# Second attention: the forget gates enter the scores by DMA, GpSimd and VectorE's maximum pass, not by TensorE products

## The reference

```
log_f = log_sigmoid(h @ w_f + b_f)            # one value per token and head
c     = cumsum(log_f, axis=tokens)
s     = (q * 64**-0.5) @ k.T + c[query] - c[key]
s     = where(key <= query, s, -1e30)
o     = softmax(s) @ v
```

## Time and profile before

| | us |
|---|---|
| median of 3 runs | 2159.78 |
| lowest, highest | 2157.82, 2160.03 |
| the profiled execution, device time | 2159.29 |
| its span on the core | 2157.5 |
| PE busy | 2127.7 (99%) |
| DVE busy | 1006.3 (47%) |
| ACT busy | 879.4 (41%) |
| POOL busy | 936.5 (43%) |

### The profile page before, as it was taken

How to read it: one execution, slowest core, us unless ns; L and a number is a source line. 1 busy time by engine, 2 the same in 40 slices (tenths; PEclk the granted TensorE clock), 3 DMA queues, 4 the chain that set the end, 5 groups by cost and what they waited for, 6 DMA issues and landing times.

```text
span 2157.5 us, 25220 instructions
## 1 busy us (share of the span) xinstructions
PE 2127.7 (99%) x10070; PEld 1739.1 (81%) x10070; DVE 1006.3 (47%) x1790; ACT 879.4 (41%) x1365; POOL 936.5 (43%) x424
## 2 busy tenths in 40 slices
PE   9999999999999999999999999999999999999998
PEld 7877778888888887777778888888888888888886
DVE  5887865265525235666635322314633254223134
ACT  5444455344424254555434422324522244223234
POOL 5632124444444455222235444445544454444446
PEclk9999999999999999999999999999999999999999
DMA  4421113333333332211122333332223323333322
GB/s 161 147 87 41 49 50 98 94 102 98 98 98 98 97 109 79 69 51 57 50 88 79 97 98 98 98 97 87 90 92 96 96 79 98 97 98 98 98 86 80
DMA packets 53829, 193.26 MB, mean 90 GB/s; under 512 B 6096, under 2 KB 6224, under 8 KB 53712
## 3 DMA queue, kind: packets, MB, share of 16 engines
q1 hardware_dynamic: 52992, 189.81, 28.3%
q10 hardware_dynamic: 720, 1.84, 0.3%
HBM read 189.53 MB, written 2.10 MB: 89 GB/s over the span
## 4 chain that ended last, share of the span: by engine, by line
PE 90%; DVE 5%; ACT 4%; issue 1%; POOL 0%; DMA 0%; DVEq 0%; ACTq 0%; POOLq 0%
PE ps L518 28%; PE ps L520 27%; PE ps L519 27%; PE ps L730 1%; ACT w_hi L1862 1%; PE ps L983 1%; PE ps L1002 1%; PE ps L722 1%; PE ps L712 1%; PE ps L614 1%; PE ps L1009 1%; DVE xg_lo L1173 1%; PE ps L1011 0%; PE ps L1010 0%; ACT fprob L2001 0%
## 5 line engine op out<-in xcount | busy, mean ns | idle before, releaser
L471 POOL TENSOR_TENSOR w_lo<-w_raw,w_hi 128x1024 fp32r<-128x1024 f32 x352 | 854.2, 2428 | 1182.6 <-ACT w_hi L1862 1182.5
L518 PE MATMUL ps<-xg_hi,w_hi 128*128 128x512 f32 x1688 | 675.1, 400 | 4.9 <-POOL w_lo L485 2.6
L520 PE MATMUL ps<-xg_hi,w_lo 128*128 128x512 f32 x1688 | 659.4, 391 | 0.0
L519 PE MATMUL ps<-xg_lo,w_hi 128*128 128x512 f32 x1688 | 658.7, 390 | 0.0
L1862 ACT ACTIVATE w_hi<-w_raw 128x1024 fp32r<-128x1024 f32 x352 | 372.0, 1057 | 626.1 <-PE ps L520 623.0
L518 PEld LDWEIGHTS ps<-xg_hi,w_hi 128*128 128x128 f32 x1688 | 317.6, 188 | 79.6 <-issue 12.4
L520 PEld LDWEIGHTS ps<-xg_hi,w_lo 128*128 128x128 f32 x1688 | 317.4, 188 | 68.0
L519 PEld LDWEIGHTS ps<-xg_lo,w_hi 128*128 128x128 f32 x1688 | 318.0, 188 | 59.6
L518 PE MATMUL ps<-h_hi,w_hi 128*128 128x512 f32 x688 | 267.6, 389 | 0.0
L519 PE MATMUL ps<-h_lo,w_hi 128*128 128x512 f32 x688 | 267.6, 389 | 0.0
L520 PE MATMUL ps<-h_hi,w_lo 128*128 128x512 f32 x688 | 267.6, 389 | 0.0
(11 more groups left out here) (342 smaller groups left out, 2425.3 us busy)
## 6 DMA issues: line engine op xcount, KB each, us to landing
w_raw<-in_weights SPq DMA_DIRECT2D x352, 512.0 KB, 3.5
out_x<-mixed SPq DMA_DIRECT2D x8, 256.0 KB, 2.1
resid<-in_x SPq DMA_DIRECT2D x3, 512.0 KB, 7.9
p_raw<-in_p ACTq DMA_DIRECT2D x3, 512.0 KB, 3.5
resid<-in_x SPq DMA_DIRECT2D x2, 256.0 KB, 4.2
last_gain<-in_last_gain SPq DMA_DIRECT2D x1, 512.0 KB, 4.4
w_raw<-in_weights SPq DMA_DIRECT2D x1, 256.0 KB, 3.6
w_raw<-in_weights ACTq DMA_DIRECT2D x1, 256.0 KB, 3.8
```

Source lines behind the costliest of these rows:

```text
L471: pool.tensor_tensor(w_lo[:, slot, :], w_raw[:, u % RAW, :], w_hi[:, slot, :].bitcast(F32), ALU.subtract).then_inc(w_ready, 1)
L518: pe.matmul(o, w, x, start=start, stop=False)
L519: pe.matmul(o, w, xl, start=False, stop=False)
L520: return pe.matmul(o, wl, x, start=False, stop=stop)
```

## The change

`c_head`, `c_hi`, `ones_r` and `head_sel` go, and with them everything that makes them. After the running sum ACT stores the 16 rows of `c_rows` to a tensor in device memory. For each pair, ACT then issues four DMAs (`gates_to_rows`), one for each query block: block qi reads the first (qi + 1) * 128 gates of both heads of the pair and writes them to all 128 partitions of `gate_row[:, :, qi]`, so that they end at column 512. For pair 0 that is ahead of ACT's work on units 144 and later; for pair p + 1 it stands where line 2270 stood. POOL adds the causal triangle to the last 128 columns of the eight rows of a partition in one operation (`gate_rows`), after it has waited for all four DMAs. It does so behind `low` of fixed units: behind unit fox + 6 for pair 0, and behind fox + 10, 13, 15, 18, 20, 23 and 25 for pairs 1 to 7 (fox is unit 141). DVE's `mx` takes `gate_row` in place of `causal`. The wait for `crow` moves from TensorE, ahead of `scores(0)`, to DVE, ahead of `mx(0)`. `scores` stops after its three products.

```diff
-        ones_r = sb("ones_r", [P, P], F32R)
...
-        head_sel = sb("head_sel", [P, 8], whole_lines=False)
...
-            c_hi = sb("c_hi", [P, S], F32R, fx)
-            c_head = sb("c_head", [P, S], F32R, fx)
+            gate_row = sb("gate_row", [P, 2, QB, S], scope=fx)
...
+        c_dram = nc.dram_tensor("c_dram", (16, S), F32, kind="Internal").ap()
...
-            pool.memset(head_sel[:], 0.0).then_inc(c_pool, 1)
...
-            for n, (first, base) in enumerate(((0, 0), (32, 0), (64, -1), (96, -1))):
-                rows = head_sel[first:first + 32, :]
-                pool.wait_ge(c_pool, 10 + n)
-                pool.affine_select(out=rows, in_=rows, compare_op=ALU.not_equal, fill=1.0, base=base,
-                                   pattern=[[-2, 8]], channel_multiplier=1).then_inc(c_pool, 1)
...
+            def gate_rows(p):
+
+                own_block = gate_row[:, :, :, S - P:S].rearrange("p h q s -> p (h q) s")
+                pool.wait_ge(A2["clanded"], 64 * (p + 1))
+                pool.tensor_tensor(own_block, own_block, causal[:, S - P:S].unsqueeze(1).to_broadcast([P, 2 * QB, P]),
+                                   ALU.add).then_inc(A2["crow"], 1)
+
+            gates_after = {U["fox"] + 6: 0, **{U["fox"] + fox_made(p, 3) // DC + RING: p + 1 for p in range(7)}}
...
                     low(u)
+                    if u in gates_after:
+                        gate_rows(gates_after[u])
...
-                            pe.matmul(ps[:, 2 + hd, 0:n], a[rows, :], b[rows, 0:n], start=t == 0, stop=False)
-                    for hd in range(2):
-                        rows = slice(hd * HD, (hd + 1) * HD)
-                        pe.matmul(ps[:, 2 + hd, 0:n], ones_r[rows, :], c_head[rows, 0:n], start=False, stop=True).then_inc(A2["scores"], 1)
+                            mm = pe.matmul(ps[:, 2 + hd, 0:n], a[rows, :], b[rows, 0:n], start=t == 0, stop=t == 2)
+                            if t == 2:
+                                mm.then_inc(A2["scores"], 1)
...
                 pe.wait_ge(bank_free, u0 + 3 * p + 2)
-                pe.wait_ge(A2["crow"], p + 1)
...
-            dve.wait_ge(s_fg["act"], 4)
-            dve.wait_ge(s_fg["dve"], 4)
-            for first in (32, 96):
-                rows = slice(first, first + 32)
-                low(c_rows[rows, :], c_rows[rows, :], c_hi[rows, :], s_fg["dve"])
-            dve.wait_ge(s_fg["dve"], 6)
-
-            dve.tensor_scalar(c_head[:], c_rows[:], head_sel[:, 0:1], None, ALU.mult).then_inc(A2["crow"], 1)
...
-                        masked_peak(A2, fstat, fprob, qi, hd)
+                        masked_peak(A2, fstat, fprob, qi, hd, gate_row[:, hd, qi, :])
...
+                dve.wait_ge(A2["crow"], p + 1)
                 mx(0)
...
-            act.activation(ones_r[:], ones[:], ACT.Copy).then_inc(c_act, 1)
...
+            def gates_to_rows(p):
+
+                for qi in range(QB):
+                    n = (qi + 1) * P
+                    act.dma_start(gate_row[:, :, qi, S - n:S], c_dram[2 * p:2 * p + 2, 0:n].unsqueeze(0).to_broadcast([P, 2, n])).then_inc(
+                        A2["clanded"], 16)
+
             act.wait_ge(s_fg["dve"], 4)
-            act.activation(c_hi[:], c_rows[:], ACT.Copy).then_inc(s_fg["act"], 1)
+            act.dma_start(c_dram, c_rows[0:16, :]).then_inc(c_stored, 16)
+            highs(u0 + 7)
+            act.wait_ge(c_stored, 16)
+            gates_to_rows(0)
...
                 if p < 7:
-                    act.activation(c_head[:], c_rows[:], ACT.Copy, scale=head_sel[:, p + 1:p + 2]).then_inc(A2["crow"], 1)
+                    gates_to_rows(p + 1)
```

More of the change, by code:

```diff
@@ L252, in build @@
         token = sb("token", [P, 14], whole_lines=False)
-        head_sel = sb("head_sel", [P, 8], whole_lines=False)
-        sb("rest_of_line", [P, 8], whole_lines=False)
+        sb("rest_of_line", [P, 16], whole_lines=False)
         m1 = ExitStack()
@@ L373, in build @@
         s_cs = stage_sems("cmp_att", "scores", "sub", "exp", "stat", "probs")
-        A2 = stage_sems("fox", *att_names, "qk", "qkhi", "vturned", "vhi", "vlo", "crow")
+        A2 = stage_sems("fox", *att_names, "qk", "qkhi", "vturned", "vhi", "vlo", "crow", "clanded")
+        c_stored = sem("c_stored")
+        c_dram = nc.dram_tensor("c_dram", (16, S), F32, kind="Internal").ap()
         s_fg = stage_sems("forget", "dve", "act")
@@ L441, in _ @@
             pool.memset(valid[:], 1.0).then_inc(c_pool, 1)
-            pool.memset(head_sel[:], 0.0).then_inc(c_pool, 1)
             pool.memset(own[:], 1.0).then_inc(c_pool, 1)
-            pool.wait_ge(c_pool, 6)
+            pool.wait_ge(c_pool, 5)
             pool.affine_select(out=ident[:], in_=ident[:], compare_op=ALU.not_equal, fill=1.0, base=0,
@@ L465, in _ @@
                                    pattern=[[0, HD]], channel_multiplier=(-1, 1)[g]).then_inc(c_pool, 1)
-            pool.wait_ge(c_pool, 16)
+            pool.wait_ge(c_pool, 11)
             def low(u):
@@ L630, in _ @@
                 pe.matmul(ps[:, 0, 0:P], ones[:], ones[:], start=True, stop=True)
-            pe.wait_ge(c_pool, 16)
+            pe.wait_ge(c_pool, 11)
             u0 = U["cmp_in"]
@@ L791, in values @@
                 head_values(A1, event(b) + kb, kb, vv_hi[:, :, b % 2], vv_lo[:, :, b % 2], b % 2 == 0 and kb == 0, b % 2 == 1 and kb == QB - 1)
-            pe.wait_ge(c_act, 4)
+            pe.wait_ge(c_act, 3)
             pe.wait_ge(s_kv["lo"], 6)
@@ L1190, in _ @@
             dve.wait_ge(gain_loaded, 16)
-            dve.wait_ge(c_pool, 16)
+            dve.wait_ge(c_pool, 11)
             for m in range(DC):
@@ L1320, in _, with masked_peak @@
             scaled(U["gates"], T[:, 0:1, :])
-            def masked_peak(A, st, pr, qi, hd):
+            def masked_peak(A, st, pr, qi, hd, mask):
                 n = (qi + 1) * P
-                dve.tensor_tensor_reduce(pr[:, hd, P_OFF[qi]:P_OFF[qi] + n], ps[:, 2 + hd, 0:n], causal[:, QB * P - n:], -1.0, BIG,
+                dve.tensor_tensor_reduce(pr[:, hd, P_OFF[qi]:P_OFF[qi] + n], ps[:, 2 + hd, 0:n], mask[:, QB * P - n:], -1.0, BIG,
                                          ALU.add, ALU.min, st[:, 0, hd, qi:qi + 1]).then_inc(A["peak"], 1)
@@ L1345, in head_peaks @@
                 for hd in range(2):
-                    masked_peak(A, st, probs, qi, hd)
+                    masked_peak(A, st, probs, qi, hd, causal)
             def head_normalise(A, s, qi, st, probs, gate=None):
@@ L1915, in _ @@
             act.wait_ge(vec_loaded, 16)
-            act.wait_ge(c_pool, 16)
+            act.wait_ge(c_pool, 11)
             highs(4)
```

## The result

The changed kernel takes 2170.8 us (median of 4, 2169.99 to 2173.09), the kernel before beside it 2158.8: a ratio of 1.0058, 95% interval 1.0046 to 1.0070, 12 us slower. The forecast was 2169 in a range of 2160.5 to 2178.

The account below looks back on a forecast made before the run. TensorE, with 90% of the chain of waits, was taken as the bound. -4.0 (products) + 4.9 (pair 0) + 5.6 (ACT's issues) + 2.8 (pair 2) = +9.3 us, 2169 on the median, range 2160.5 to 2178.

Parts of the forecast that it names:

- the three losses: Pair 0's chain to the first maximum 4.9 us, ACT's four issues 5.6, POOL's late add in pair 2 2.8.
- The gate products: TensorE's stream: dropping them saves 0.62 us a pair, 5.0 for eight, of which 4.0 is kept.
- The start of the program: POOL's dropped memset and selections and DVE's dropped head work gain 0 us, 0.3 if misjudged.
- Pair 0: Store, gate DMAs and POOL's add make the first maximum 3.9 us late; one caught scaling adds 1.0; together 4.9.
- ACT's issues: Four issues per pair replace one copy, delaying w_hi by 1.0 us in pairs 0, 1, 2, 3, 5; sum 5.6.
- Pair 2: POOL's add behind fox + 13 comes late, the first maximum waits 3.6 us, TensorE loses 2.8.
- The other pairs' adds: POOL's adds from pair 3 on come ahead of need or within TensorE's slack: 0 us.
- The rival in which issues and gates hide: ACT issues cost 2.0 us, gates land at 882 (0.9), pair 2 stays (2.8): 2161.5; chance 0.17.
- The rival in which the products are all there is: TensorE's stream alone decides, new arrivals fit its slack, 5.0 us gained: 2154.8; chance 0.05.
- The slow one: Packet-bound gates landing at 891 or issues of twice the length: +15 or +21, 2175 to 2181 us; chance 0.16.
- A maximum pass slower for its other mask: DVE's maximum pass loses from reading another mask; same shapes in SBUF, so no chance of its own.

Follow-up runs that it names:

- e1: Kernel before with only the fourth (gate) product left out of the scores, c_head still made: 2156.6 us, ratio 0.9991.
- e2: Changed kernel with POOL's add for pair 2 one unit earlier, behind fox + 12 in place of fox + 13: 2166.3 us.
- e4: Changed kernel with POOL's add for pair 0 behind the low half of fox + 8 in place of fox + 6: 2168.9 us.
- e5: Changed kernel with pair 0's add in four parts, each waiting for its own DMA, each maximum only for its part: 2167.5 us.
- e3: Changed kernel with the 28 gate DMAs of pairs 1 to 7 issued from SyncE's queue in place of ACT's: 2166.1 us.
- e8: Changed kernel with 13 idle matmuls filling TensorE's wait ahead of the second scores of pair 0: 2169.6 us.
- e6: Changed kernel with the changes of e2, e3 and e5 together: 2158.9 us, ratio 1.0003 to the kernel before.
- e9: Changed kernel, but pair 0 keeps the fourth product; pairs 1 to 7's gate DMAs issued by SyncE, pair 2's add one unit earlier: 2156.7 us, ratio 0.9990.

## Why the prediction was right

The forecast was +9.3, the result +12.0, within the range and of the right sign. The sign was earned: each of the three losses that it named was found in its place. Set out as its terms, the distances give -1.8 for the products (e1), +6.7 in pair 0, +3.1 for all else that the change adds in pairs 1 to 6 (e2 against e1), and +3.9 for the late place in pair 2 with its clock (changed against e2), 11.9 of 12.0. By its own steps:

- **The gate products, 4.0 gained: mis-sized.** e1 gives 1.7. The groups do leave the stream at 0.11 to 0.23 us each, and TensorE is 0.66 ahead by the end of the scores. Its error lies in taking this saving for kept: I had struck only the places where TensorE already waited for a maximum, and not asked whether the probabilities and turned blocks behind the scores would come earlier too. In pair 1 they came 0.66 - 0.42 = 0.24 less early than the scores, for DVE's scaling ran into POOL's `low`. Pairs 1, 2, 4 and 5 were to give 0.62 each and gave 0.3, 0.7, 0.4 and 0.3; pair 2, with no collision and no wait, is the only one that kept all.
- **The start of the program, 0: right.** The first scores stood at 882.1 to 883.4 in all profiles, with and without the selections.
- **Pair 0, 4.9 by itself, 5.7 with its ACT share and kept saving: right in kind, 6.7 measured.** The first maximum came at 887.11, with the program 0.9 ahead of the kernel before, so 4.3 late where I said 3.9: the store landed after 1.6 and not 2.1, the gates 9.1 after the first issue and not 7.8, the add took 2.35 and not 2.7. Of scalings caught by a `low` I counted one, 1.0 us; two were caught, 1.0 and 1.7. e4 (0.29 each) and e5 (one caught) show that cause. Of the 6.7, 0.8 belong to the one profile; e2, e3 and e8 have 5.9, which is nearer to the 5.7.
- **ACT's issues, 5.6 (its parts add to 5.7): right in kind, too high.** `w_hi` comes 1.93 - 1.32 = 0.61 later than before, where I said 1.0, because the sequencer issues the first two ahead. Against no copy and no issue it is 1.23, and that is what e3 took back in pairs 3 and 5. The forecast was against the copy, and there the runs give about half: TensorE's waits for the low half of turned probabilities grow by 2.4 (3.7 to 6.1, where I said about 9), and of the 3.1 above about 2 are such waits, 0.6 each in pairs 2, 3 and 5. Pair 1, for which I had said 1.0, gives 0.1 to 0.2. That there is next to nothing in pair 4 came as said.
- **Pair 2, 2.8: right, but for the clock.** 3.0 by e3 against e6, for the reason given, and 0.9 more for the clock, which the prediction left out altogether. The text ahead of it says that nothing hangs on the clock, since it was full before; that holds for the kernel before and not for the changed one. In pair 0 the clock stayed full when idle matmuls filled the wait (e8). In pair 2 its fall followed the wait in four kernels (changed, e4, e5, e8) and not in e3, and that the wait caused it is not shown.
- **The other pairs' adds, 0: right for TensorE.** In pair 1 the add is in time. In pair 4 the first maximum waits for it (998.41, the add ends at 998.38) and comes 0.3 later than in the other pairs; TensorE's distance stays at 25.0, as the forecast said of its slack, though e1 has 24.7 there.

The products were sized 2.3 us too favourably, pair 0 and the clock too cheaply, and ACT's issues too dearly. These errors partly cancel, so that the total came within 3 us is partly luck.

The rival in which issues and gates hide (2161.5) fell by the landing, by the two caught scalings and by the 1.12 us that ACT stands idle at its issues. The rival in which the products are all there is (2154.8) fell with the maximum of pair 2. The slow one fell by the landing too: 884.67, with the program 0.9 ahead, is 885.6 in the old times and not 891, and the issues were 0.49 apart and not twice that. Its packets took 64 ns (an estimate: 1.9% - 0.3% of 16 x 2169 us over 8736 packets), under half of the weights' 184. A maximum pass slower for its other mask is ruled out: 0.29 us at 128 keys with either.

The Trainium skill, page DMA: Bandwidth & Descriptors, section "Anatomy of one DMA", gives a DMA about 2.0 us plus its bytes over 436 GB/s, a fit made on DMAs that GpSimd issues. By it, as an estimate, 1.31 MB would land some 5 us after the issue. The runs show 9.1 from the first issue and 7.65 for the last DMA of 512 KB, so the measurement decides against it here. The Trainium skill, page SBUF — State Buffer, section "Who interferes with whom", says of the port pair that VectorE in a two-port mode shares with GpSimd that whoever comes first has it for the whole instruction and the other is blocked. The trace agrees, with 2.38 us for a scaling of 0.29 that began 0.08 us behind a `low` and ended 0.08 us behind its end.

## What to carry to other kernels

Work taken off the busiest engine is worth only what its partners can follow: test it first by leaving the work out. That test is one small edit, and here it shows 1.7 us of 5.0, less than any of the three losses. When an operation goes to another engine's ordered stream, look up when the item ahead of it runs in each round; one round of eight was wrong here and cost 3.9 us. A full clock before a change is no promise for the kernel after it, if the change adds waits to TensorE. The DMA route paid here only for rounds that were prepared a round ahead; the first round, with nothing to hide under, kept the direct way (e9).

## What the runs showed of the hardware

- A DMA that copies two rows of memory to all partitions in pieces of 512 to 2048 bytes was slow to land: 3.6, 5.0, 6.3 and 7.7 us for 128, 256, 384 and 512 KB, issued in this order 0.49 us apart, beside 3.5 for a plain load of 512 KB. How much of the later ones is waiting behind the earlier was not separated.
- ACT's sequencer issued a DMA 0.10 us before the exponential ahead of it in program order began, but four issues in a row came 0.49 apart, and 1.12 us of ACT's time passed idle for them.
- A scaling on DVE that met GpSimd's `low` ended just behind it: 2.38, 2.01 and 1.32 us in place of 0.29 (e5, changed kernel), 1.04 in place of 0.49 (e1).
- TensorE's wait of 3.42 us in pair 0 was followed by a granted clock of 0.64 and then 0.50, and the same code with idle matmuls in the wait had 1.00. A wait of 2.33 us in pair 2 was followed by 0.77 in one kernel and by 1.00 in another, so whether it falls is not settled by the wait alone; the runs don't say by what. Pair 0 shows the same: behind a wait of 2.25 us in e5 the clock was 1.00 between 886 and 894, behind one of 1.89 us in e6 it was 0.57 between 890 and 894.
- What a fall costs hangs on who sets the pace: 1.5 us of TensorE's stream in pair 2 of the changed kernel, of which 0.9 reached the time, and nothing in pair 0 of e2 (32.3, as in e8 with a full clock).
